# A streamed mixture-of-experts kernel: coarser transfers late in the loop, another order of the last six products, and two moves in its first part

## The reference

```python
h = rmsnorm(x, mix_norm_g)                       # x: 256 tokens x 1024
proj = h @ w_in                                  # pooling, q, k, v, gates
x = x + (sigmoid(gate_A) * pool_branch + sigmoid(gate_B) * diff_attention_branch) @ w_out
t = rmsnorm(x, ffn_norm_g)
top_v, top_i = top_k(t @ router_w + router_b, 4) # of 32 experts
comb = one_hot_sum(top_i, softmax(top_v))
for e in range(32):
    g = minimum(t @ w_gate[e] + b_gate[e], 7.0)
    u = clip(t @ w_up[e] + b_up[e], -7.0, 7.0)
    act = (u + 1.0) * (g * sigmoid(1.702 * g))
    out = out + comb[:, e:e+1] * (act @ w_down[e] + b_down[e])
x = x + out
```

## Time and profile before

| | before |
|---|---|
| median of 3 runs | 1079.12 us (1078.42 to 1079.86) |
| the profiled execution | 1078.32 us, its span 1076.0 us |
| TensorE busy | 1046.0 us, 97% of the span |
| VectorE, ScalarE, GpSimd busy | 272.9, 199.7, 40.4 us |
| moved by the transfers | 433.65 MB, 403 GB/s over the span |
| granted clock of TensorE, mean | 0.996 of full speed |

### The profile page before, as it was taken

How to read it: one execution, slowest core, us unless ns; L and a number is a source line. 1 busy time by engine, 2 the same in 40 slices (tenths; PEclk the granted TensorE clock), 3 DMA queues, 4 the chain that set the end, 5 groups by cost and what they waited for, 6 DMA issues and landing times.

```text
span 1076.0 us, 12286 instructions
## 1 busy us (share of the span) xinstructions
PE 1046.0 (97%) x5121; PEld 445.2 (41%) x5121; DVE 272.9 (25%) x548; ACT 199.7 (19%) x348; POOL 40.4 (4%) x55
## 2 busy tenths in 40 slices
PE   9999999999999999999999999999999999999997
PEld 5899984333333333333333333333333333333332
DVE  6876753111111111111111111111111011111121
ACT  4667522111111101111111111111111011111011
POOL 0460020000000000000000000000000000000000
PEclk9999999999999999999999999999999999999999
DMA  9835999999999999999999999999999999999997
GB/s 313 307 124 163 406 392 378 409 426 428 440 427 431 429 432 432 432 431 434 429 431 432 432 434 430 432 431 430 434 434 430 432 431 430 425 429 429 429 421 282
DMA packets 37947, 433.65 MB, mean 403 GB/s; under 512 B 5109, under 2 KB 7962, under 8 KB 20122
## 3 DMA queue, kind: packets, MB, share of 16 engines
q1 hardware_dynamic: 37280, 432.64, 95.9%
q10 hardware_dynamic: 634, 0.56, 0.2%
HBM read 432.14 MB, written 1.05 MB: 403 GB/s over the span
## 4 chain that ended last, share of the span: by engine, by line
PE 70%; DMA 25%; ACT 3%; DVE 1%; issue 0%; DVEq 0%
PE ps L1063 45%; DMA ring<-in_exp_w_up 22%; PE ps L951 4%; PE ps L691 4%; PE ps L692 4%; PE ps L693 4%; DMA arena<-in_exp_w_up 3%; PE ps L1011 3%; ACT arena L1382 2%; PE ps L1000 1%; PE ps L1071 1%; PE ps L757 1%; PE ps L819 0%; PE ps L968 0%; PE ps L705 0%; ACT ring_r L1244 0%
## 5 line engine op out<-in xcount | busy, mean ns | idle before, releaser
L1063 PE MATMUL ps<-ring,arena 128*64 128x512 f32 x2432 | 543.3, 599 | 12.4 <-DMA ring<-in_exp_w_up 12.1
L1063 PEld LDWEIGHTS ps<-ring,arena 128*64 128x64 f32 x2432 | 168.2, 137 | 337.0 <-issue 313.5
L1063 PE MATMUL ps<-arena 128*64 128x512 f32 x640 | 142.0, 595 | 2.1 <-DMA arena<-in_exp_w_up 1.9
L1880 DVE TENSOR_SCALAR arena<-ps 128x512 f32<-128x512 f32 x30 | 20.8, 692 | 464.4 <-PE ps L1063 464.4
L1382 ACT COPY arena<-ps 128x512 f32<-128x512 f32 x31 | 32.5, 1048 | 255.9 <-PE ps L951 255.9
L1063 PEld LDWEIGHTS ps<-arena 128*64 128x64 f32 x640 | 44.0, 137 | 86.5 <-issue 81.5
L1893 DVE TENSOR_SCALAR arena<-ps 128x512 f32<-128x512 f32 x31 | 21.4, 692 | 177.2 <-PE ps L1063 177.2
L1011 PE MATMUL ps<-arena 64*128 64x512 f32 x256 | 63.9, 616 | 0.0
L1422 ACT COPY arena<-ps 128x256 f32<-128x256 f32 x30 | 11.2, 372 | 279.3 <-PE ps L1011 279.3
L691 PE MATMUL ps<-ring_r 128*128 128x256 f32 (+1 forms) x192 | 59.1, 308 | 0.4 <-DVE arena_r L1682 0.3
L951 PE MATMUL ps<-arena 128*64 128x512 f32 x248 | 58.5, 592 | 0.0
(11 more groups left out here) (245 smaller groups left out, 673.0 us busy)
## 6 DMA issues: line engine op xcount, KB each, us to landing
ring<-in_exp_w_up SPq DMA_DIRECT2D x19, 4096.0 KB, 31.9
ring<-in_exp_w_down SPq DMA_DIRECT2D x18, 4096.0 KB, 31.3
ring<-in_exp_w_gate SPq DMA_DIRECT2D x18, 4096.0 KB, 32.5
ring<-in_exp_w_up SPq DMA_DIRECT2D x10, 2048.0 KB, 39.6
ring<-in_exp_w_down SPq DMA_DIRECT2D x10, 2048.0 KB, 38.9
ring<-in_exp_w_gate SPq DMA_DIRECT2D x10, 2048.0 KB, 40.3
arena<-in_exp_w_gate SPq DMA_DIRECT2D x5, 4096.0 KB, 32.5
arena<-in_exp_w_down SPq DMA_DIRECT2D x5, 4096.0 KB, 34.0
```

The costliest lines, as they stand in the source:

```text
L1063: last = mm(ps[BLOCK * to:BLOCK * (to + 1), bank, :], src[:, c, half, :], moved, start=(fresh and half == 0 and c == 0), stop=(half == 1 a ...
L1880: v.tensor_scalar(g1, ps[:, 4, :], LIMIT, None, ALU.min).then_inc(g_ready, 1)
```

## The change

Five edits.

1. `FINE` goes from `E - 5` to `E - 2`: the matrices of experts 27, 28 and 29 come in one transfer each, and SP's loop runs over one step more in place of written-out issues. TensorE's waits in the loop lose the term for a halved last step.
2. The order of the last six products becomes gate, up of 30, gate, up of 31, down of 30, down of 31. The last up and the down of 30 come in four transfers, the last down in five as before.
3. In that order the turn of the last weights moves into up of 31 (before chunk 4), the two turns of the last activation into down of 30 (before chunks 3 and 5), and the two scatters of expert 30 into down of 31 (before chunks 3 and 5), which takes bank 5. ACT copies the result of expert 30 after the turned activation instead of before.
4. `spread_norm` gives its first transpose to `turn_columns`, which stays before chunk 4 of the first q product; the rest, with its waits, goes before chunk 6.
5. The pick of expert 0 for the second 128 tokens is made straight from the rank's sums in PSUM and from a weight made beforehand (`first_weight`); `rank(1)` follows it.

```diff
-        FINE = E - 5
-        GATE30, UP30, GATE31, DOWN30, UP31, DOWN31 = range(PAIR, PAIR + 6)
-        TAIL = {DOWN30: (0, 2, 4, 6, 8), UP31: (0, 2, 4, 6, 7, 8), DOWN31: (0, 2, 4, 6, 7, 8)}
+        FINE = E - 2
+        GATE30, UP30, GATE31, UP31, DOWN30, DOWN31 = range(PAIR, PAIR + 6)
+        TAIL = {UP31: (0, 2, 4, 6, 8), DOWN30: (0, 2, 4, 6, 8), DOWN31: (0, 2, 4, 6, 7, 8)}
...
-                with sp.Fori(1, STEPS - 1) as step:
+                with sp.Fori(1, STEPS) as step:
...
             def spread_norm():
...
                             if t == 0 and c == 4:
                                 turn_x(1, 0)
                                 turn_x(1, 1)
+                                turn_columns()
+                            if t == 0 and c == 6:
                                 spread_norm()
...
-                            elif not isinstance(step, int):
-                                if halved(PASS * (STEPS - 1) + n):
...
+                            elif halved(n, rolled=not isinstance(step, int)):
...
                 product(r, 0, GATE31, 4, last_h_in, [(3, lambda: turn_results(i))])
-                pe.wait_ge(actT_ready, i + 1)
-                product(r, 0, DOWN30, 7, actT, fresh=True)
-                pe.wait_ge(weights_ready, r + 1)
-                turn_weights(6)
...
                 pe.wait_ge(pickT_ready, i + 2)
                 biases(1, 5, next_e)
-                product(r, 0, UP31, 5, last_h_in)
-
-                pe.wait_ge(y_ready, i + 2)
-                scatter_tile(0, y_e, pickT)
-                pe.wait_ge(act_first, r + 1)
-                turn_part(0, 4).then_inc(turn_first, 1)
-                scatter_tile(1, y_e, pickT).then_inc(rows_down, 1)
-                pe.wait_ge(act_ready, i + 2)
-                pe.wait_ge(pickT_ready, i + 3)
-                turn_part(1, 6).then_inc(act_T, 1)
+                product(r, 0, UP31, 5, last_h_in, [(4, last_weights)])
+                pe.wait_ge(actT_ready, i + 1)
+                product(r, 0, DOWN30, 7, actT, [(3, first_turn), (5, second_turn)], fresh=True)
                 pe.wait_ge(actT_first, r + 1)
-                product(r, 0, DOWN31, 7, last_actT, [(2, rows_turned)], fresh=True)
+                product(r, 0, DOWN31, 5, last_actT, [(2, rows_turned), (3, first_rows), (5, second_rows)], fresh=True)
...
             dve.wait_ge(chosen_ready, 2)
+            own(v.tensor_tensor(first_weight, chosen[:, 1, 0:1], rstd[:, 1:2], ALU.mult))
             dve.wait_ge(rank_done, 2)
+            v.tensor_scalar(pick[:, 1, :], iota, ps[:, 2, 0:1], first_weight, ALU.is_equal, ALU.mult).then_inc(first_pick, 1)
             rank(1)
-            select_tile(1, 0).then_inc(first_pick, 1)
```

More of the change, by code:

```diff
@@ L248, in build @@
         ss_more = small[:, 186:187]
+        first_weight = small[:, 187:188]
         ss2 = small[:, 196:200].rearrange("p (t h) -> p t h", t=NT)
@@ L270, in build @@
         down30_in = [sem(f"down30_in{i}") for i in range(2)]
-        up31_in = [sem(f"up31_in{i}") for i in range(3)]
+        up31_in = [sem(f"up31_in{i}") for i in range(2)]
         down31_in = [sem(f"down31_in{i}") for i in range(5)]
@@ L472, in build @@
         PAIR = MATRICES * (E - 2)
-        FINE = E - 5
-        GATE30, UP30, GATE31, DOWN30, UP31, DOWN31 = range(PAIR, PAIR + 6)
-        TAIL = {DOWN30: (0, 2, 4, 6, 8), UP31: (0, 2, 4, 6, 7, 8), DOWN31: (0, 2, 4, 6, 7, 8)}
-        TAIL_IN = {DOWN30: [quarter_in[DOWN30 % HOLDS][0], down30_in[0], quarter_in[DOWN30 % HOLDS][1], down30_in[1]],
-                   UP31: [quarter_in[UP31 % HOLDS][0], up31_in[0], quarter_in[UP31 % HOLDS][1], up31_in[1], up31_in[2]],
-                   DOWN31: down31_in}
+        FINE = E - 2
+        GATE30, UP30, GATE31, UP31, DOWN30, DOWN31 = range(PAIR, PAIR + 6)
+        TAIL = {UP31: (0, 2, 4, 6, 8), DOWN30: (0, 2, 4, 6, 8), DOWN31: (0, 2, 4, 6, 7, 8)}
+        TAIL_IN = {n: [quarter_in[n % HOLDS][0], seconds[0], quarter_in[n % HOLDS][1], seconds[1]]
+                   for n, seconds in ((UP31, up31_in), (DOWN30, down30_in))}
+        TAIL_IN[DOWN31] = down31_in
         def tail_count(signal, r):
@@ L495, in matrix @@
                 return divmod(n, MATRICES)
-            return ((E - 2, 0), (E - 2, 1), (E - 1, 0), (E - 2, 2), (E - 1, 1), (E - 1, 2))[n - PAIR]
+            return ((E - 2, 0), (E - 2, 1), (E - 1, 0), (E - 1, 1), (E - 2, 2), (E - 1, 2))[n - PAIR]
         h_split = tuple(ring_r[seat[H_SLOT]][:, NC * S * i:NC * S * (i + 1)].rearrange("p (c s) -> p c s", c=NC)
@@ L609, in load_round @@
                     load_matrix(r, 0, n)
-                with sp.Fori(1, STEPS - 1) as step:
+                with sp.Fori(1, STEPS) as step:
                     for n in range(PASS):
                         load_matrix(r, step * UNROLL, n)
-                for n in range(PASS * (STEPS - 1), MATRICES * E):
+                for n in range(PASS * STEPS, MATRICES * E):
                     load_matrix(r, 0, n)
@@ L719, in _, with turn_columns @@
             turn_x(0, 1)
-            def spread_norm():
+            def turn_columns():
                 pe.wait_ge(rows_in, 16 * 4)
@@ L724, in spread_norm @@
                    ident[R_BGATE:R_ROWS, R_BGATE:R_ROWS]).then_inc(cols_T, 1)
+            def spread_norm():
                 pe.wait_ge(con_rest, 16)
@@ L1045, in product @@
                                            + 16 * (n // HOLDS + 1))
-                            elif not isinstance(step, int):
-                                if halved(PASS * (STEPS - 1) + n):
[L1048 to L1052, removed]
+                            elif halved(n, rolled=not isinstance(step, int)):
+                                pe.wait_ge(lower_in[at], r * (16 * lowers(at, MATRICES * E)) + step * (16 * lowers(at, PASS))
+                                           + 16 * lowers(at, n + 1))
                         row = hold_chunks(at)[:, half, c, :]
@@ L1147, in last_pair, with last_weights, first_turn, second_turn @@
                 product(r, 0, GATE31, 4, last_h_in, [(3, lambda: turn_results(i))])
-                pe.wait_ge(actT_ready, i + 1)
-                product(r, 0, DOWN30, 7, actT, fresh=True)
-                pe.wait_ge(weights_ready, r + 1)
-                turn_weights(6)
+                def last_weights():
+                    pe.wait_ge(weights_ready, r + 1)
+                    turn_weights(6)
+                def first_turn():
+                    pe.wait_ge(act_first, r + 1)
+                    turn_part(0, 4).then_inc(turn_first, 1)
+                def second_turn():
+                    pe.wait_ge(act_ready, i + 2)
+                    pe.wait_ge(pickT_ready, i + 3)
+                    turn_part(1, 6).then_inc(act_T, 1)
+                def first_rows():
+                    pe.wait_ge(y_ready, i + 2)
+                    scatter_tile(0, y_e, pickT)
+                def second_rows():
+                    scatter_tile(1, y_e, pickT).then_inc(rows_down, 1)
+                def rows_turned():
+                    pe.wait_ge(actT_ready, i + 2)
                 pe.wait_ge(pickT_ready, i + 2)
                 biases(1, 5, next_e)
-                product(r, 0, UP31, 5, last_h_in)
-                pe.wait_ge(y_ready, i + 2)
-                scatter_tile(0, y_e, pickT)
-                pe.wait_ge(act_first, r + 1)
-                turn_part(0, 4).then_inc(turn_first, 1)
-                scatter_tile(1, y_e, pickT).then_inc(rows_down, 1)
-                pe.wait_ge(act_ready, i + 2)
-                pe.wait_ge(pickT_ready, i + 3)
-                turn_part(1, 6).then_inc(act_T, 1)
+                product(r, 0, UP31, 5, last_h_in, [(4, last_weights)])
+                pe.wait_ge(actT_ready, i + 1)
+                product(r, 0, DOWN30, 7, actT, [(3, first_turn), (5, second_turn)], fresh=True)
                 pe.wait_ge(actT_first, r + 1)
-                def rows_turned():
-                    pe.wait_ge(actT_ready, i + 2)
-                product(r, 0, DOWN31, 7, last_actT, [(2, rows_turned)], fresh=True)
+                product(r, 0, DOWN31, 5, last_actT, [(2, rows_turned), (3, first_rows), (5, second_rows)], fresh=True)
                 def last_scatter(t, q):
@@ L1439, in last_pair @@
                 fn(sig, g1, ACT.Sigmoid, scale=ALPHA).then_inc(sig_ready, 1)
-                act.wait_ge(piece_done, pieces + 2 * (DOWN30 + 1))
-                nc.scalar.copy(y_e, ps[:, 7, :]).then_inc(y_ready, 1)
                 act.wait_ge(pick_T, i + 2)
@@ L1448, in last_pair @@
                 nc.scalar.copy(turned[:, 2 * P:], ps[:, 6, 2 * P:]).then_inc(actT_ready, 1)
+                act.wait_ge(piece_done, pieces + 2 * (DOWN30 + 1))
+                nc.scalar.copy(y_e, ps[:, 7, :]).then_inc(y_ready, 1)
                 act.wait_ge(piece_done, pieces + 2 * (DOWN31 + 1))
-                nc.scalar.copy(last_y[:, 0:HALF // 2], ps[:, 7, 0:HALF // 2]).then_inc(y_first, 1)
-                nc.scalar.copy(last_y[:, HALF // 2:], ps[:, 7, HALF // 2:]).then_inc(y_ready, 1)
```

(2 more changed lines are left out.)

## The result

| | before | after |
|---|---|---|
| median | 1078.95 us, 20 runs (1077.83 to 1080.78) | 1080.48 us, 20 runs (1078.82 to 1082.71) |
| the profiled execution | 1078.32 us, span 1076.0 us | 1080.19 us, span 1077.9 us |
| granted clock of TensorE, mean | 0.996 | 0.994 |

The ratio is 1.0015, its interval 1.0009 to 1.0021: slower by 1.5 us, within the 0.2% that was called no change. Predicted were 1080.2 us and "same".

A forecast was written before the change was run, and what follows sets the result against it. Transfers and TensorE were nearly tied, with TensorE alone setting the new tail: 2.8 us late, 1.7 us of holes recovered, +1.1 us on 1079.12 us, so 1080.2 us; range 1077.9 to 1082.1 us.

The forecast's parts named there:

- Up 29 whole, TensorE 2.8 us late: Expert 29's up starts at 997.4 us behind its whole transfer, ends 2.8 us late; gate 31 starts at 1036.5 us.
- A second transfer costs 0.07 us: Experts 27 to 29: halving a matrix takes 9.79 us against 9.72, so each extra transfer costs 0.07 us.
- Rival D: A split costs more than 0.07 us; up 29 would land 1.8 us earlier still, 1078.4 us; chance 0.04.
- The holes are used up and give 1.7 us back: Tail from gate 31: TensorE's waits for landing pieces, 1.7 us in before, go with the new order.
- The 32.9 us of work: TensorE's work from gate 31 to the end of the last down: 34.6 us less 1.7 us of holes.
- the sum: All parts together: tail ends at 1069.4 us against 1068.29, start unmoved, so +1.1 us.
- With TensorE in time, the order would cost +0.3 us: Last down: third chunk at 1061.4 us, then six chunks and two scatters, ending at 1068.6 us, +0.3.
- rival B: TensorE is in time after all and the tail ends on the landing: 1078.1 to 1079.4 us; chance 0.17.
- The lower bound of the tail: Last landing plus one chunk, 1067.3 us, -1.0 us: the tail cannot end earlier.
- rival A: As summed: TensorE comes late out of expert 29 and the holes are used up, 1080.2 us; chance 0.54.
- The clock in up 29: Rival: the clock falls in expert 29's up behind its wait, adding 1.7 us: +2.8, 1081.9 us; chance 0.20.
- The first part: Spread of the norms later: cost 0. Pick from the rank's sums: gain 0 to 0.07 us, taken as 0.

The follow-up runs named there:

- e5: after with every matrix from number 5 on by halves, 75 more transfers; 1084.93 us, ratio 1.0056.
- e2: before with whole transfers for experts 27 to 29 as its only edit, old order and first part; 1079.65 us, ratio 1.0007.
- e1: after with the transfers of experts 27 to 29 by halves again, new order and first part kept; 1080.28 us, ratio 1.0014.
- e7: e1 without expert 30's two scatters, a matmul of eight columns standing in, so the output lacks that expert's part; 1078.78 us, ratio 1.0001.
- e3: before with only the later spread of the norms and the pick from the rank's sums; 1079.05 us, ratio 1.0002.
- e6: e1 with expert 30's scatters before chunks 2 and 4 of the last product instead of 3 and 5; 1079.73 us, ratio 1.0007.
- e4: after with only expert 29 in halves, experts 27 and 28 whole; 1080.22 us, ratio 1.0010.
- after_look_1: after unchanged, one more profiled execution, in which the clock fell in up 28; 1079.99 us.
- after_look_4: after unchanged, a fourth further profiled execution, in which the clock fell in up 29; 1081.41 us.

## Why the prediction was right

*Up 29 whole, TensorE 2.8 us late.* Right. Gate 31 starts 126.59 us behind up 26 instead of 123.76, +2.83 us, and up 29 itself is where it was put, to 0.05 us.

*A second transfer costs 0.07 us.* Right, by e5 (0.06 to 0.08) and by the 0.60 us that eight whole matrices gain. Rival D falls.

*The holes are used up and give 1.7 us back.* The holes do go, but the size was off and the cause was put in the wrong place. The size: from gate 31 to the end of the last product it takes 33.23 us instead of 34.60, 1.37 us back and not 1.7. The 32.9 us of work that I left over after the holes are 32.6 us in the old order (e2) and 33.2 in the new one: the holes were 2.0 us, and the breaks of 0.6 us that the new order puts inside the products were left out of the sum. 2.83 us less 1.37 gives +1.46 for the +1.1 of the sum. The cause: I let the new order close the holes. e2 shows that the late TensorE closes them in the old order too, and better.

*With TensorE in time, the order would cost +0.3 us* (the case between the bounds, and the ground of rival B). Wrong. e1 has TensorE in time and costs 1.56 us, 0.96 with whole landings. I had taken the third chunk at 1061.4 us, and that piece does land there (1063.29 in e1 less its shift of 1.39 and less 0.60, 1061.3); but what follows takes 7.8 us, not 7.2: two scatters of 1.06 us and two breaks in the product. The lower bound of the tail, -1.0 us, took the last landing plus one chunk; in e7, without any scatter and less the stand-in and the 0.60 us of whole landings, it is 0.27 - 0.32 - 0.60 = -0.65 us, because the third piece binds before the last. Rival B, 1078.1 to 1079.4 us, falls by e1: TensorE is in time there and the median is 1080.28 us. It did not hurt the forecast, since TensorE is late in after; but late or in time, the new order ends at nearly the same place (72.25 and 72.35). So the time alone did not confirm rival A against B, and had TensorE been in time, 1080.2 us would have been met by luck. What confirms A are the starts of up 29 and gate 31 and the missing waits.

*The clock in up 29.* Its chance was put at 0.20; one of five profiled executions shows it. The 20 timed runs of after reach 1082.71 us and those of before 1080.78, and how many of them had the fall no trace says. The width alone is no sign of it: e1, with halves at up 29, reaches 1081.65 us.

*The first part.* Nothing and nothing, as e3 and the starts at 170.18 and 173.00 us say.

Of the whole, then: whole transfers alone cost 0.86 us, the new order alone 1.56, both together 1.46. They don't add up, because each pays with the same thing, TensorE's time between the landings of the last pieces. No version tried here is faster than before: e3 is the same, and e6 has the shortest tail of those with the new order and all of the output.

## What to carry to other kernels

At the end of a stream ask of each of the last pieces what work lies behind its landing, since the largest of landing plus work left is the bound; work that doesn't need these pieces belongs ahead of them, where TensorE waits anyway. Splitting a transfer of a deep queue costs 0.07 us here and pays only where TensorE has no slack left behind it, as at up 29: with experts 27 to 29 split, gate 31 starts 2.8 us earlier and in the old order the program ends 0.86 us earlier. To split expert 29 alone (e4) comes too late, since TensorE has already waited for a whole up 28. Ahead of a slack neither a whole transfer nor a fall of the clock costs anything (after_look_1).

## What the runs showed of the hardware

Behind the same wait of 1.7 us TensorE's clock sometimes falls and sometimes doesn't: in the five executions of after there are 39 such waits at ups from 700 us on, and 17 of the products behind them took 8.78 us instead of 7.09, with the clock for some of that time at 1.2 and not 2.4 GHz, as in after_look_4. In all profiles but e5's it is 35 of 84; in e1 one of seven. Before the fall and before the absence of one the engine had done the same work: ahead of the wait at up 29, from 990 to 996 us, it is busy for 6.00 of 6.00 us with 29 instructions both in after, where no fall follows, and in after_look_4, where one does. A product that fell uses up the next wait. Where the wait is shared between two halves (0.5 and 1.24 us, e5), no half of any up took longer than 3.65 us, and the mean granted clock was 0.999. The Trainium skill (TensorE: Matmul & The Clock Gate, HAM oscillation) describes a loop, with longer waits than these, in which every wait for a transfer starts the next tile cold; here, at 17 of 39, the trace agrees only in part.

The stream of transfers stands up to 2.4 us apart between executions by the up of expert 26, while the first weight product differs by 1.1 us at most and not in step with it (172.78 us in e1, whose up 26 is at 911.31; 172.83 in before, 909.93). What moves it was not found.
